# Up product of quarters 1 to 3: eight tiles as two groups of seven block products instead of one group and four whole tiles

## The reference, cut to what matters

```
h2 = rmsnorm(x, pre_norm_mlp)
y = square(relu(h2 @ w_up)) @ w_down        # w_up 1024 x 4096, w_down 4096 x 1024
x = x + rmsnorm(y, post_norm_mlp)
```

## Time and profile before

| | |
|---|---|
| median of the runs | 922.54 us (922.27 to 922.78) |
| the profiled execution | 922.09 us |
| its span | 920.8 us |
| PE busy in the span | 907.7 us |
| DVE busy | 681.2 us |
| ACT busy | 505.9 us |

### The profile page before, as it was taken

One profiled execution on the slowest core, in us unless ns is written; L12 is line 12 of the kernel. 1 busy time (PEld: TensorE's weight loads), 2 busy tenths in 40 slices (PEclk: granted clock), 3 DMA queues, 4 the chain that ended last, 5 costly groups with the idle time before them and its releaser, 6 DMA issues.

```text
span 920.8 us, 13893 instructions
## 1 busy us (share of the span) xinstructions
PE 907.7 (99%) x5234; PEld 748.4 (81%) x5234; DVE 681.2 (74%) x1171; ACT 505.9 (55%) x917; POOL 126.9 (14%) x134
## 2 busy tenths in 40 slices
PE   9999999999999999999999999999999999999997
PEld 7778777777898777777777889987898889889876
DVE  6668859888749787766664751879768956976897
ACT  6455447356555355644544324578857546634754
POOL 2002403431040001100000313000000010000015
PEclk9999999999999999999999999999999999999999
DMA  7222112112232411212212355453763485276546
GB/s 254 94 90 70 47 58 82 47 47 81 96 111 95 162 47 55 78 55 78 67 50 73 110 186 180 161 183 77 225 179 98 130 230 178 50 239 174 172 96 167
DMA packets 30067, 107.52 MB, mean 117 GB/s; under 512 B 3505, under 2 KB 4465, under 8 KB 29489
## 3 DMA queue, kind: packets, MB, share of 16 engines
q1 hardware_dynamic: 25008, 87.13, 28.2%
q0 software_dynamic: 4272, 12.91, 8.0%
q10 hardware_dynamic: 720, 6.59, 1.9%
HBM read 94.04 MB, written 6.29 MB: 109 GB/s over the span
## 4 chain that ended last, share of the span: by engine, by line
PE 75%; DVE 15%; ACT 5%; issue 3%; DMA 1%; SPq 0%; DVEq 0%; ACTq 0%
PE PB L488 9%; PE PB L489 9%; PE PB L490 9%; PE PB L1116 5%; PE PB L1117 5%; PE PB L1118 5%; PE PB L695 4%; DVE wl L1778 3%; PE PB L732 2%; PE PB L1088 2%; PE PB L1087 2%; PE PB L1086 2%; PE PB L935 2%; PE PB L936 2%; PE PB L937 2%
## 5 line engine op out<-in xcount | busy, mean ns | idle before, releaser
L488 PE MATMUL PB<-hh,wh 128*128 128x512 f32 x480 | 197.1, 411 | 0.2 <-DVE X L2309 0.2
L1778 DVE TENSOR_TENSOR wl<-raw,wh 128x1024 fp32r<-128x1024 f32 (+2 forms) x108 | 137.2, 1270 | 68.2 <-ACT wh L1179 67.9
L490 PE MATMUL PB<-hh,wl 128*128 128x512 f32 x480 | 187.4, 390 | 0.0
L489 PE MATMUL PB<-hl,wh 128*128 128x512 f32 x480 | 187.3, 390 | 0.0
L1179 ACT ACTIVATE wh<-raw 128x1024 fp32r<-128x1024 f32 (+2 forms) x108 | 110.2, 1024 | 65.2 <-PE PB L490 14.4
L1179 ACT ACTIVATE wh<-AR 128x1024 fp32r<-128x1024 f32 x71 | 75.1, 1059 | 66.3 <-PE PB L1118 44.3
L1778 DVE TENSOR_TENSOR wl<-AR,wh 128x1024 fp32r<-128x1024 f32 x71 | 87.6, 1236 | 31.1 <-ACT wh L1179 30.7
L488 PEld LDWEIGHTS PB<-hh,wh 128*128 128x128 f32 x480 | 90.1, 188 | 24.8 <-issue 7.2
L490 PEld LDWEIGHTS PB<-hh,wl 128*128 128x128 f32 x480 | 90.1, 188 | 19.5
L489 PEld LDWEIGHTS PB<-hl,wh 128*128 128x128 f32 x480 | 90.3, 188 | 18.8 <-issue 1.9
L1347 ACT ACTIVATE S<-S,sm 128x256 f32<-128x256 f32 (+3 forms) x96 | 50.6, 528 | 96.6 <-DVE sm L1881 72.5
(11 more groups left out here) (462 smaller groups left out, 2062.3 us busy)
## 6 DMA issues: line engine op xcount, KB each, us to landing
AR<-in_dn SPq DMA_DIRECT2D x40, 512.0 KB, 5.2
raw<-in_w2g SPq DMA_DIRECT2D x16, 512.0 KB, 3.4
raw<-in_upe SPq DMA_DIRECT2D x16, 512.0 KB, 3.6
AR<-in_ub POOLq DMA_DIRECT2D x12, 512.0 KB, 6.0
raw<-in_w1e SPq DMA_DIRECT2D x10, 512.0 KB, 3.4
raw<-in_w1q SPq DMA_DIRECT2D x8, 512.0 KB, 3.4
x_kept<-X ACTq DMA_DIRECT2D x2, 2048.0 KB, 7.9
raw<-in_woab SPq DMA_DIRECT2D x8, 512.0 KB, 3.5
```

What stands on the lines that cost most here:

```text
L488: e.matmul(bank[:], a[:, col(k)], xa[:, k, :], start=k == 0, stop=False)
L489: e.matmul(bank[:], a[:, col(k)], xb[:, k, :], start=False, stop=False)
L490: i = e.matmul(bank[:], b[:, col(k)], xa[:, k, :], start=False, stop=k == 7)
L1778: e.tensor_tensor(wl[c % 3][:, 0:n], raw_of(c), wh[c % 3][:, 0:n].bitcast(F32), ALU.subtract).then_inc(*up("lo", c))
```

## The change

Tiles 4 to 7 of quarters 1 to 3 are made as a second group (g = 1) of seven block products too, in other PSUM banks and from other weight slots. The opening has 18 steps in place of 13, and the two chunks of down product 0 lie inside it; a quarter has 28 steps in place of 25. Group 0's block sums get two buffers of their own (`WE`), group 1's use slot "b". Every down chunk jj waits for the features of its own group. The first quarter keeps its whole tiles; the inputs' factors for products 4 and 7 are kept in `hh` and `hl`, and three of the steps that make them move a few steps ahead. PSUM banks of the down products change with the table `DOWN_BANKS`. The core of the diff, with the order written for ACT, DVE, POOL and SP:

```diff
...
-OPENING = (("p", 1), ("d", 12), ("p", 5), ("d", 13), ("p", 2), ("p", 6), ("m", 4), ("p", 7), ("p", 3), ("p", 4),
-           ("m", 5), ("m", 6), ("m", 7))
+OPENING = (("p", 0, 1), ("d", 12), ("p", 0, 5), ("d", 13), ("p", 0, 2), ("p", 0, 6), ("p", 1, 5), ("p", 0, 7),
+           ("p", 0, 3), ("p", 0, 4), ("p", 1, 1), ("p", 1, 2), ("p", 1, 6), ("d", 0), ("p", 1, 7), ("p", 1, 3),
+           ("p", 1, 4), ("d", 1))
 
...
+DOWN_BANKS = ((7, 2), (6, 3), (1, 0), (7, 2), (6, 3), (4, 5), (1, 0))
+UP_BANKS = ((6, 7, 2), (0, 1, 3))
+ODD = ("bl1", "t3")
...
             if PLAN[c][0] == "ub":
-                return slot("a", int(PLAN[c][1] % 8 in (1, 7)))
+                g, r = divmod(PLAN[c][1] % 16, 8)
+                return slot("b", int(r in (1, 7))) if g else WE[int(r not in (1, 7))][:]
...
                 if r in (1, 2, 5):
-                    up_bank[r], before = tenant({1: 2, 5: 3, 2: 4}[r], {1: "bl1", 5: "v12", 2: "v11"}[r], q)
-                bank = up_bank[{1: 1, 6: 1, 7: 1, 4: 1, 5: 5, 3: 5, 2: 2}[r]]
+                    up_bank[g, r], before = tenant({1: x, 5: y, 2: z}[r], {1: ODD[g], 5: "v12", 2: "v11"}[r], q, g)
+                bank = up_bank[g, {1: 1, 6: 1, 7: 1, 4: 1, 5: 5, 3: 5, 2: 2}[r]]
...
                 if jj == 0:
-                    down_bank[n] = [tenant(2 * (n % 3) + s, *summed(q, n, s)) for s in range(2)]
+                    down_bank[n] = [tenant(DOWN_BANKS[n][s], *summed(q, n, s)) for s in range(2)]
...
                 c = piece(q, n, jj)
                 a, b = wh[c % 3], wl[c % 3]
                 e.wait_ge(*to("lo", c))
-                if q and jj == 0:
-                    e.wait_ge(*to({0: "bl0", 1: "bl1", 2: "tw1", 3: "tw0", 4: "tw2", 5: "bl2", 6: "tw3"}[n], q))
+                if q:
+                    e.wait_ge(*to({0: "bl0", 1: "bl1", 2: "tw1", 3: "tw0", 4: "tw2", 5: "bl2", 6: "tw3"}[n], q, jj))
...
+            def kept(q, g, r):
+
+                e.wait_ge(*to("gemm", product(q, g, r)))
+                if (q, g) == (1, 0):
+                    e.wait_ge(*to("bl", 0, 3, 1))
+                else:
+                    readers = {1: ("t0", "bl0"), 5: ("v22",), 6: ("t0", "t2") if g else ("tw1", "t3"),
+                               7: ("tw1", "t3") if g else ("bl2", "t1")}[r]
+                    for event in readers:
+                        e.wait_ge(*to(event, *((q, 0) if g else (q - 1, 1))))
+                bank = seat["v12" if r == 5 else ODD[g], q, g]
+                e.activation(tmp[{1: 0, 6: 1, 7: 2, 5: 3}[r]][:], bank[:], ACT.Copy).then_inc(*up("pc", q, g, r))
...
             for q in range(1, 4):
                 for b, c in enumerate(beats(q)):
                     if b == 6:
-                        kept(q, 6)
+                        kept(q, 0, 6)
                     if b == 8:
-                        kept(q, 7)
+                        kept(q, 0, 7)
                     if b == 9:
-                        squared(q, 2)
+                        squared(q, 0, 2)
                     if b == 10:
-                        squared(q, 1)
+                        squared(q, 0, 1)
+                    if b == 11:
+                        kept(q, 1, 1)
+                    if b == 13:
+                        kept(q, 1, 6)
+                    if b == 15:
+                        kept(q, 1, 7)
+                    if b == 17:
+                        squared(q, 1, 1)
+                    if b == 18:
+                        hidden_high(q, 1, 1)
                     if c + 2 < len(PLAN):
                         hi(c + 2)
...
                     if b == 1:
-                        kept(q, 1)
+                        kept(q, 0, 1)
                     if b == 3:
-                        kept(q, 5)
+                        kept(q, 0, 5)
                     if b == 6:
-                        squared(q, 0)
+                        squared(q, 0, 0)
...
                     if b == 7:
-                        hidden_high(q, 0)
+                        hidden_high(q, 0, 0)
                     if b == 9:
-                        squared(q, 3)
+                        squared(q, 0, 3)
+                        kept(q, 1, 5)
                     if b == 10:
-                        hidden_high(q, 2)
-                        mix_high(q, 0)
-                        relu(q, 4)
-                        mix_high(q, 2)
+                        hidden_high(q, 0, 2)
+                        mix_high(q, 0, 0)
                     if b == 11:
-                        mix_high(q, 1)
-                        hidden_high(q, 1)
-                        relu(q, 5)
-                        mix_high(q, 3)
+                        mix_high(q, 0, 2)
                     if b == 12:
-                        relu(q, 6)
-                        mixed(q, 2)
+                        mix_high(q, 0, 1)
                     if b == 13:
-                        relu(q, 7)
+                        squared(q, 1, 0)
+                        hidden_high(q, 0, 1)
+                        mix_high(q, 0, 3)
                     if b == 14:
-                        mixed(q, 3)
-                    if (q, b) == (3, 15):
-                        e.wait_ge(*to("gemm", product(3, 4)))
+                        hidden_high(q, 1, 0)
+                    if b == 16:
+                        squared(q, 1, 3)
+                        squared(q, 1, 2)
+                    if b == 17:
+                        mix_high(q, 1, 0)
+                    if b == 18:
+                        mix_high(q, 1, 1)
+                        mix_high(q, 1, 2)
+                    if b == 20:
+                        mix_high(q, 1, 3)
+                        hidden_high(q, 1, 2)
+                    if (q, b) == (3, 20):
+                        e.wait_ge(*to("gemm", product(3, 1, 4)))
                         e.activation(unit, ident, ACT.Copy).then_inc(*up("tri", 2))
...
                 if i == 3:
-                    e.wait_ge(*to("rb", q, 1))
-                    e.wait_ge(*to("t1", q))
-                    e.wait_ge(*to("tw0", q))
-                    x, y = seat["bl1", q], tmp[2]
-                e.tensor_tensor(MIX[i][:], x[:], y[:], ALU.subtract).then_inc(*up(f"t{i}", q))
...
+                    e.wait_ge(*to("rb", q, g, 1))
+                    if g:
+                        e.wait_ge(*to("bh1", q, g))
+                    e.wait_ge(*to("t1", q, g))
+                    e.wait_ge(*to("tw0", q, g))
+                    x, y = seat[ODD[g], q, g], MIX[g][1]
+                e.tensor_tensor(MIX[g][i][:], x[:], y[:], ALU.subtract).then_inc(*up(f"t{i}", q, g))
...
             for q in range(1, 4):
                 for b, c in enumerate(beats(q)):
-                    n = b - 13
-                    if n > 1:
-                        added(q, n // 2 - 1, n % 2)
                     if b == 8:
-                        odd_tokens(q)
+                        odd_tokens(q, 0)
                     if b == 9:
-                        even_tokens(q, 2)
+                        even_tokens(q, 0, 2)
                     if b == 10:
-                        mix(q, 0)
-                        mix(q, 2)
-                    if b == 11:
-                        mix_low(q, 0)
-                        mix(q, 3)
+                        mix(q, 0, 0)
+                        mix(q, 0, 2)
+                    if b == 12:
+                        even_tokens(q, 1, 1)
+                    if b == 15:
+                        odd_tokens(q, 1)
+                    if b == 16:
+                        even_tokens(q, 1, 2)
+                    if b == 17:
+                        mix(q, 1, 0)
+                    if b == 18:
+                        hidden_low(q, 1, 1)
                     if c + 2 < len(PLAN):
                         lo(c + 2)
...
+                    if b in (2, 3):
+                        third(q, b - 2)
...
                     if b in (4, 5):
                         added(q - 1, 6, b - 4)
                     if b == 5:
-                        even_tokens(q, 1)
+                        even_tokens(q, 0, 1)
+                    if b in (6, 7):
+                        second(q, b - 6)
                     if b == 7:
-                        hidden_low(q, 0)
-                    if b in (10, 11):
-                        third(q, b - 10)
-                    if b == 10:
-                        hidden_low(q, 2)
-                        mix(q, 1)
+                        hidden_low(q, 0, 0)
                     if b == 11:
-                        mix_low(q, 2)
-                        mix_low(q, 1)
-                        hidden_low(q, 1)
-                        hidden(q, 4)
-                        mix_low(q, 3)
+                        hidden_low(q, 0, 2)
+                        mix(q, 0, 1)
+                        mix_low(q, 0, 0)
                     if b == 12:
-                        second(q, 0)
-                        hidden(q, 5)
-                        mixed(q, 2)
+                        mix_low(q, 0, 2)
```

(128 more changed lines are left out.)

240 lines of the change are left out of this document (112 added, 128 removed).

## The result

| | before | after |
|---|---|---|
| median | 922.66 us (922.27 to 922.85) | 939.69 us (938.53 to 941.39) |
| profiled execution, its span | 922.09, 920.8 us | 941.39, 940.1 us |
| start of the span to the first p(0,1) | 664.42 | 664.15 |
| quarters 1, 2, 3 (first product to first product; the third up to the last transposes) | 81.15, 80.30, 80.88 | 83.10, 88.83, 85.54 |
| last transposes to the end | 14.05 | 18.48 |

The ratio is 1.0187, with a 95% interval of 1.0174 to 1.02: 17.0 us slower, where 5 were forecast. The profiled execution is the slowest of the four after, so its span differs from that of before by more, 19.3 us: -0.3 ahead, +1.95, +8.53 and +4.66 in the quarters, +4.4 at the end.

What follows compares the result with a forecast made beforehand. PE's matmul count was taken to bound quarters 1 to 3 while ACT and DVE keep up. Saved matmuls, late places and weight sums made 246.3 against 240.9 us, +5.4: 922.1 + 5.4 = 927.5 us, range 920 to 937.

Steps and rivals of the forecast that it cites:

- PE's own work: PE in quarters 1 to 3: 78.4 us a quarter after against 80.1 before, saving 1.7 to 1.9 if nothing waits.
- The 3.5 us a quarter beside it: Alternative saving in PE's work from the skill's 109 ns per 256-column matmul; set aside for the row's 120 ns.
- The two late places: PE waits for DVE 1.5 us before d1/1 and 0.67 inside d2/0: 2.1 us a quarter, even with weights in time.
- The weight sums: Block sums by DMA landing late for their hi: quarters of 81.0, 84.7 and 80.6 us, from 80.5 without late sums.
- L: Time from the end of one lo until its block sum lands: taken as 6.2, 7.6 and 5.8 us by quarter.
- the walk: ACT and DVE queues followed through the new order at row prices; the old order gave 80.2 us against 80.3 read.
- Rival 3: Three sums issued within 4 us at a quarter's start crowd each other: L 8, 85.9 a quarter, 939 us; chance 0.12.
- I count nothing for it: PE's granted clock in quarters 1 to 3: 1.00 in the rows, so no cost was put on it falling.
- a fall of the clock in the new gaps: Stated sign of a wrong forecast: granted clock dropping in PE's new gaps; no size given.
- a wait at a block product for something other than `lo` and `kept`: Stated sign of a wrong forecast: PE held at block products by anything but these two; no size given.
- The tile banks change places: nothing: PSUM banks of the tiles swapped by the change: claimed to cost nothing.
- The tail keeps its work: The kernel's end, after the quarters: claimed to keep its work, with no time added in the sum.

Runs made afterwards that it cites:

- e11: e9 with both product 4 additions in quarter 3's step 26, their follow-up additions behind the last lo, ACT's first weights in step 26: 920.13 us, ratio 0.9975.
- e4: Kernel after with only the order of ACT and DVE around steps 16 to 19 changed: 932.17 us, ratio 1.0116.
- e8: Kernel after with GpSimd's sums at a quarter's start in the order p(0,7), wait for the block and p(1,5), p(0,6): 939.84 us, ratio 1.0188.
- e10: Kernel after with the two plain loads of slot d moved behind the lo of p(0,6): 939.82 us, ratio 1.0189.
- e12: e11 without e1's edit, so GpSimd's order is that of the kernel after: 929.23 us, ratio 1.0078.
- e3: Kernel after with the token sums written to PSUM bank 3 in place of bank 2: 939.24 us, ratio 1.0186.
- e5: Kernel after with quarter 3's additions of down products 1 to 3 reordered, mix_low(1,3) in step 23, ACT's first weight in step 25: 938.73 us, ratio 1.018.
- e1: Kernel after with GpSimd's sums for p(0,7) and p(0,6) ahead of the block wait and p(1,5)'s sum: 930.93 us, ratio 1.0089.
- e6: Kernel after with the edits of e1, e3, e4 and e5 together: 921.3 us, ratio 0.9986.
- e9: e6 with both banks of product 1 added in quarter 3's step 21, mix_low(1,2) in step 22, hidden_low(1,2) in step 24: 923.8 us, ratio 1.0016.

## Why the prediction was wrong

**PE's own work: right.** 78.4 forecast, 78.67 in e11, 2.87 to 2.88 a product. The 240.9 us for before is three times one quarter; by the marks of the table above it is 242.3, with 0.9 more in quarter 1 and 0.6 in quarter 3. The 3.5 us a quarter beside it (by the Trainium skill, "TensorE: Matmul & The Clock Gate", section "Back-to-back issue gap") set the formula's 2.62 us a product against the row's 5.45 for a tile. The same formula on both sides (5.18 us a tile) makes it 2.4, an estimate.

**The two late places: right in place, and in size to 0.6 us.** 2.1 us a quarter forecast; 2.05, 1.9 and 2.75 measured (6.7 in all); undone alone they give 7.5 us (e4), in which the gaps before p(0,6) were other ones too.

**The weight sums: the step that failed.** "Eight sums a quarter in place of four, with about as many plain loads, can only lengthen L; I leave it where it was, for want of a row." That a late sum makes `hi`, `lo` and so PE late was right. The size of L and the place were wrong: L was put at 6.2, 7.6 and 5.8 us for every sum, and the sum for p(0,6) in quarters 2 and 3 landed in 14.1 and 11.3, so that PE waited 5.1 and 2.35 us at p(0,6), where the walk had no wait. The waits that the walk did give for a long L (p(1,3), d0/1, 3.0 at d1/1) are not in the kernel after, where p(1,3)'s sums took 5.46 and 5.73 us in these quarters. They came in e8 and e10, where these took 6.6 to 7.5 us in the same quarters: d0/1 0.5 and d1/1 2.6 us. Rival 3 had named the cause, three sums at a quarter's start, and at 0.12 was held too unlikely. That it came near the time is luck: its 85.9 a quarter makes 257.7 for the three, against 257.5, but quarter 1 took 83.10 and quarter 2 88.83, its L of 8 was too small, and it had neither the half clock nor the end. What would have told: the order of POOL's program. The wait for `block_even1` stands ahead of a sum that was ready 3 us earlier, and the rows had two such sums apart, never three with four plain loads out beside them. The DMA engines' time that a sum takes could have been read from the trace of before, as shown above. By e12 against e11 this term is 9.1 us; I had given sums 4.8.

The Trainium skill, "DMA: Bandwidth & Descriptors", section "Anatomy of one DMA — SWDGE (gpsimd) path", gives 2.0 us plus the bytes at 436 GB/s for one DMA, an estimate of 3.2 us for 512 KB. The smallest sum here took 5.1 us, so the measurement decides.

**"I count nothing for it": the clock.** It costs what the gap before it did not: 2.4 us in p(0,6) and 0.35 in the next product of quarter 2. In quarters 1 to 3 of all runs, product or down steps behind a wait of 1.8 to 2.35 us ran at full clock (2.85 and 2.98 us: after, e12) or partly at half (4.09: e4; 4.47: e3). Those behind 2.4 to 3.4 us took 1.3 to 2.4 us more (4.17 to 5.29), but for one in e10 behind 2.59 us, and those behind 1.7 us or less never did. The forecast had named a fall of the clock in the new gaps as a sign of its being wrong, and a wait at a block product for something other than `lo` and `kept` as another; both came.

**"The tile banks change places: nothing": wrong by 1.0 us**, since the bank of the token sums changed with them (quarter 1; e3, e8). In quarter 3 another 1.0 went at p(1,5), whose bank DVE had still to add into `acc`: `added` stood behind the `lo` that waited.

**"The tail keeps its work": true, and no answer.** It kept its work and lost its place: 4.4 us, since `added` of products 1 to 3 moved behind other operations of DVE. e5 and e11 give back 2.6 and 1.5 of it. Why e11's end is still 2.9 us longer than before's is open; PE waits 1.8 us in it for `raw` from DVE (3.3 after), and before has no such wait.

Summed for the profiled execution: without gaps 236.9 us for the three quarters (e11), late places 6.7, gaps before p(0,6) 7.5, half clock behind the first 2.75, the two waits behind a late `lo` 2.1, and 1.5 by which the steps around all these waits grew beyond them give 257.5, against 242.3 before; with the end's 4.4 and -0.3 ahead, 19.3. The forecast of 927.5 is 13.9 us short of this execution: 9.8 in the quarters (15.2 against 5.4), 4.4 at the end, -0.3 ahead.

## What to carry over

Read the order of every queue that issues transfers, and list for each moment how many are out and what they cost the DMA engines: a wait for a load ahead of ready work turns one late transfer into three that collide. A late transfer's price is its gap, the half clock behind it, and whatever stands in order behind the instruction that waits. Spreading transfers (e10) only helps if the place they move to is empty.

## What the runs showed of the hardware

- A DMA that adds 512 KB from DRAM onto SBUF took 5.1 us at the least and 5.3 to 8.0 in the kernel before; 9.1 to 11.1 where it went out 0.5 us behind another (e1, e6, e9, e11); 7.7 to 14.1 as the second or third of three in quarters 2 and 3. It used twice the DMA engines' time per MB of a plain load (5.5 against 2.7 us after, 6.2 against 2.9 before).
- In quarters 1 to 3, waits of PE of 1.7 us or less left the granted clock at 1.00; the shortest wait with half clock behind it was 1.90 us (e4), the longest with full clock 2.59 (e10).
- While GpSimd ran a TENSOR_TENSOR, DVE's additions over SBUF took 2.6 to 2.9 us instead of 0.7 (e5, e6, e9). The Trainium skill, "SBUF — State Buffer", section "SBUF: two separate sides", has a DVE instruction with two SBUF inputs contend with a GpSimd instruction that reads SBUF, and the later one fully blocked. The traces agree: in e9 GpSimd's pair ran from 901.59 to 904.42 us, and DVE's addition, begun at 902.02, ended at 904.96.
